# FFN up products of 512 columns with down products two tiles behind, latent-attention weight units split by halves, products on zeros at the beginning

## The reference, cut to what matters

```python
def conv_ffn(x, w_up, conv_w, conv_b, w_down):        # 2 of them, FFN_HIDDEN = 2816
    u = x @ w_up                                       # [256, 1024] @ [1024, 2 * 2816]
    up = jnp.pad(u, ((0, 0), (half, half), (0, 0)))    # over the tokens, 3 taps
    c = conv_b
    for j in range(CONV_W):
        c = c + conv_w[j] * up[:, j:j + s]
    g, val = c[..., :FFN_HIDDEN], c[..., FFN_HIDDEN:]
    return (jax.nn.gelu(g) * val) @ w_down

def swiglu(x, w_gu, w_down):                           # 2 of them, hidden width 2752
    gate, up = jnp.split(x @ w_gu, 2, axis=-1)
    return (jax.nn.silu(gate) * up) @ w_down

def mla_mixer(x, w_dq, q_norm_g, w_uq, w_dkv, kv_norm_g, w_ukv, w_o):
    cq = rms_norm(x @ w_dq, q_norm_g)                  # latent queries, 384
    q = (cq @ w_uq).reshape(b, s, H, MLA_NOPE + MLA_ROPE)
    ckv_kr = x @ w_dkv                                 # latent keys and values, 256 + 64
    ...
    # softmax attention of 8 heads, then @ w_o
```

## Time and profile before

| | us |
|---|---|
| median of 3 runs | 1225.3 (1223.99 to 1225.78) |
| profiled execution | 1222.77 |
| its span | 1221.0 |
| TensorE busy in the span | 1170.8 (96%) |
| VectorE busy | 763.6 (63%) |
| ScalarE busy | 601.2 (49%) |

### The profile page before, as it was taken

One profiled execution on the slowest core, in us unless ns is written; L12 is line 12 of the kernel. 1 busy time (PEld: TensorE's weight loads), 2 busy tenths in 40 slices (PEclk: granted clock), 3 DMA queues, 4 the chain that ended last, 5 costly groups with the idle time before them and its releaser, 6 DMA issues.

```text
span 1221.0 us, 21499 instructions
## 1 busy us (share of the span) xinstructions
PE 1170.8 (96%) x7997; PEld 1063.0 (87%) x8011; DVE 763.6 (63%) x1070; ACT 601.2 (49%) x900; POOL 69.3 (6%) x98
## 2 busy tenths in 40 slices
PE   7999999999899989999999999999989999999997
PEld 6976999999789869999987999997977878999996
DVE  5864876776656568677767455455646756555554
ACT  5554555454555555545445434334565655334342
POOL 0201000000200020000002000001000310000000
PEclk9999999999999999999999999999999999999998
DMA  6514766566243446666554666563674015766661
GB/s 204 178 35 155 206 190 187 174 202 203 93 149 119 155 124 207 186 177 204 176 169 134 195 178 200 178 166 96 176 223 156 1 36 172 209 172 200 172 175 43
DMA packets 241058, 194.59 MB, mean 159 GB/s; under 512 B 11214, under 2 KB 223792, under 8 KB 241008
## 3 DMA queue, kind: packets, MB, share of 16 engines
q1 hardware_dynamic: 240928, 193.88, 53.3%
q10 hardware_dynamic: 80, 0.03, 0.0%
HBM read 192.84 MB, written 1.05 MB: 159 GB/s over the span
## 4 chain that ended last, share of the span: by engine, by line
PE 86%; DVE 6%; ACT 4%; DMA 2%; issue 1%; POOL 1%; SPq 0%; POOLq 0%; ACTq 0%; DVEq 0%
PE psum L584 26%; PE psum L585 25%; PE psum L586 25%; DVE lo_u L1648 1%; PE psum L1143 1%; ACT hi_u L1237 1%; DVE lo_u L1665 1%; ACT hi_u L1234 1%; POOL st L506 1%; PE psum L902 1%; PE psum L1115 1%; PE psum L815 1%; PE psum L816 1%; POOL st L503 1%; DMA raw_u<-in_cmp_v_w 1%
## 5 line engine op out<-in xcount | busy, mean ns | idle before, releaser
L584 PE MATMUL psum<-act_hi,hi_u 128*128 128x256 f32 x1712 | 486.8, 284 | 9.4 <-DVE lo_u L1648 6.0
L585 PE MATMUL psum<-act_lo,hi_u 128*128 128x256 f32 x1712 | 484.2, 283 | 0.0
L586 PE MATMUL psum<-act_hi,lo_u 128*128 128x256 f32 x1712 | 484.2, 283 | 0.0
L1665 DVE TENSOR_TENSOR lo_u<-raw_u,hi_u 128x2048 fp32r<-128x2048 f32 (+3 forms) x122 | 273.7, 2243 | 236.2 <-ACT hi_u L1243 153.3
L584 PEld LDWEIGHTS psum<-act_hi,hi_u 128*128 128x128 f32 x1712 | 326.6, 191 | 17.9 <-issue 14.3
L585 PEld LDWEIGHTS psum<-act_lo,hi_u 128*128 128x128 f32 x1712 | 326.7, 191 | 3.2
L586 PEld LDWEIGHTS psum<-act_hi,lo_u 128*128 128x128 f32 x1712 | 326.7, 191 | 0.0
L1243 ACT ACTIVATE hi_u<-raw_u 128x2048 fp32r<-128x2048 f32 x72 | 137.7, 1912 | 91.6 <-PE psum L586 81.2
L584 PE MATMUL psum<-hi_d,hid_hi 128*128 128x512 f32 (+1 forms) x352 | 138.5, 393 | 1.4 <-DVE hid_lo L1755 1.4
L585 PE MATMUL psum<-lo_d,hid_hi 128*128 128x512 f32 (+1 forms) x352 | 138.0, 392 | 0.0
L586 PE MATMUL psum<-hi_d,hid_lo 128*128 128x512 f32 (+1 forms) x352 | 137.0, 389 | 0.0
(11 more groups left out here) (245 smaller groups left out, 1201.4 us busy)
## 6 DMA issues: line engine op xcount, KB each, us to landing
raw_u<-in_ffn_w_up SPq DMA_DIRECT2D x88, 512.0 KB, 5.4
raw_d<-in_ffn_w_down SPq DMA_DIRECT2D x86, 512.0 KB, 3.5
raw_u<-in_ffn_w_gu SPq DMA_DIRECT2D x84, 512.0 KB, 5.8
raw_u<-in_diff_w_qkv SPq DMA_DIRECT2D x24, 512.0 KB, 4.6
raw_u<-in_w_in SPq DMA_DIRECT2D x24, 512.0 KB, 4.4
raw_u<-in_mla_w_o SPq DMA_DIRECT2D x8, 512.0 KB, 4.0
raw_u<-in_diff_w_o SPq DMA_DIRECT2D x8, 512.0 KB, 4.1
raw_u<-in_w_out SPq DMA_DIRECT2D x8, 512.0 KB, 4.3
```

Source lines behind the costliest of these rows:

```text
L584: pe.matmul(o, s_hi, m_hi, start=start, stop=False)
L585: pe.matmul(o, s_hi, m_lo, start=False, stop=False)
L586: return pe.matmul(o, s_lo, m_hi, start=False, stop=stop)
L1665: dve.tensor_tensor(v[0], v[1], v[2].bitcast(F32), ALU.subtract).then_inc(S("lo_u_done"), 1)
```

## The change

- **Up products.** `act_hi` and `act_lo` become halves of one tensor `act_hl`, chunk by chunk side by side. The hi weights meet both in one product of 512 columns, which fills a whole bank: hi by hi in the first 256 columns, hi by lo in the other 256 (the crossed half). The lo weights meet `act_hi` in a product of 256 columns that adds to the crossed half. ScalarE then copies the crossed half out (`cross_out`) and VectorE adds the two halves into `up_sum` in SBUF; the taps, silu and the product read `up_sum`. The bank is free for the tile two later after the sum.
- **Order.** down(t) follows up(t+2) and not up(t+1). At the end: up(20), down(18), up(21), down(19), then down(20) and down(21) for the first token half, then both for the second. Tile 21's down weights get a third slot.
- **Hidden tile.** `hid_hi` is written by ScalarE from the float32 product, no longer by VectorE as a second product; `hid_lo` of a tile is made within the next one; the down weights of a tile are split one tile later than before.
- **Latent attention.** All its units (0 to 13) are split by halves, each half as soon as it has landed (`raw_half0_`, `raw_half1_`), and TensorE begins a unit when its first half is split.
- **Beginning.** Twelve products on zeros before anything else, four between the transposes of the two token halves and six behind them.

In the diff the last two pieces are ScalarE's and VectorE's order within a tile.

```diff
-WARM = [(0, 0, 0)] + 4 * [(19, 3, 1)] + 2 * [(12, 3, 1)]
+WARM = [(0, 4, 6)] + 4 * [(19, 3, 1)] + 2 * [(12, 3, 1)]
-HALVED = sorted(FIRST + list(range(U_NV, U_HI + 1)))
+HALVED = sorted(list(range(U_F0)) + FIRST[1:] + list(range(U_NV, U_HI + 1)))
+BY_HALVES = range(U_F0)
...
+            def mm_beside(bank, n, s_hi, s_lo, m_hl, start, stop):
+                pe.matmul(psum[0:n, bank, :], s_hi, m_hl.rearrange("p a t -> p (a t)"), start=start, stop=False)
+                return pe.matmul(psum[0:n, bank, SEQ:], s_lo, m_hl[:, 0, :], start=False, stop=stop)
...
                 up(1, 1, P)
-                down(0, 0, P)
                 with pe.Fori(0, LOOPED) as b:
                     up(b * 2 + 2, 0, P)
+                    down(b * 2, 0, P)
+                    up(b * 2 + 3, 1, P)
                     down(b * 2 + 1, 1, P)
-                    up(b * 2 + 3, 1, P)
-                    down(b * 2 + 2, 0, P)
                 up(20, 0, P)
+                down(18, 0, P)
+                up(21, 1, width(f, 21))
                 down(19, 1, P)
-                up(21, 1, width(f, 21))
-                down(20, 0, P)
+                down(20, 0, P, False, [0])
                 down(21, 1, width(f, 21), True, [0])
+                down(20, 0, P, False, [1])
                 down(21, 1, width(f, 21), True, [1])
...
+            pe.wait_ge(S("zeros_set"), 1)
+            keep_warm(12)
             pe.wait_ge(S("ident_in"), 16)
...
+                    cross_out(0)
+                    if f < 2:
+                        conv_mid(0, cg)
+                        cross_out(1)
+                        act.wait_ge(S("tap_b"), at2(2 * g + 1))
+                        act.activation(gg[0:n, slot, :], cg[0:n, slot, :], ACT.Gelu_apprx_tanh).then_inc(S("gated"), 1)
+                        conv_mid(1, cv)
...
+                    act.wait_ge(S("hidden"), at(g + 1))
+                    if b is not None or g >= 2:
+                        act.wait_ge(S("used_d"), at(g - 1))
+                    act.activation(hid_hi[0:n, slot, :], hf[0:n, slot, :], ACT.Copy).then_inc(S("hid_hi_done"), 1)
...
+                    sum_up(0)
+                    if b is not None or 0 < t < 21:
+                        split_d(g - 1, b)
                     if f < 2:
+                        taps(0, cg)
+                    if n == P:
+                        sum_up(1)
+                    if b is not None or t:
+                        hidden_low(g - 1, 1 - slot, P)
```

More of the change, by code:

```diff
@@ L338, in program @@
         d_sq = junk[:].rearrange("p (b d) -> p b d", d=P)
[L339 removed]
+        d_hi, d_lo = (x[:, 0:2].rearrange("p a (c t) -> p (a c) t", t=SEQ) for x in (hi_d, lo_d))
         n_ks = ar(0, 2, NB + SEQ)
@@ L395, in load_unit @@
                 k = units[u].shape[1]
-                for k0, k1 in ((0, k // 2), (k // 2, k)):
-                    sp.dma_start(unit_view(raw_u, u)[:, k0:k1], units[u][:, k0:k1]).then_inc(S(f"raw_u{u % 2}"), 16)
+                for part, (k0, k1) in enumerate(((0, k // 2), (k // 2, k))):
+                    landed = f"raw_u{u % 2}" if u not in BY_HALVES else f"raw_half{part}_{u % 2}"
+                    sp.dma_start(unit_view(raw_u, u)[:, k0:k1], units[u][:, k0:k1]).then_inc(S(landed), 16)
             def load_up(f, t, slot, n):
@@ L703, in down @@
                     g = t + FT * f
+                    d = 2 if isinstance(t, int) and t == FT - 1 else slot
                     pe.wait_ge(S("hi_d_done"), g + 1)
@@ L711, in down @@
                             mm = mm3(psum[:, 2 * tk + c, :], hid_hi[0:n, slot, tok(tk)], hid_lo[0:n, slot, tok(tk)],
-                                     hi_d[0:n, slot, w], lo_d[0:n, slot, w], False, last)
-                    mm.then_inc(S("used_d" if TT - 1 in tiles else "first_part"), 1)
+                                     hi_d[0:n, d, w], lo_d[0:n, d, w], False, last)
+                    if TT - 1 in tiles:
+                        mm.then_inc(S("used_d"), 1)
+                    elif last:
+                        mm.then_inc(S("first_part"), 1)
                 up(0, 0, P, True)
@@ new lines, in taps @@
+                    def taps(part, buf):
+                        for tap, name in ((0, "tap_a"), (2, "tap_b")):
+                            dve.wait_ge(S("conv_mid" if tap == 0 else "tap_a"), at2(2 * g + part + 1))
+                            w = at(V_CW + (f * 3 + tap) * 44 + part * FT + t)
+                            o = slice(1, SEQ) if tap == 0 else slice(0, SEQ - 1)
+                            x = slice(0, SEQ - 1) if tap == 0 else slice(1, SEQ)
+                            dve.scalar_tensor_tensor(buf[0:n, slot, o], up_sum[0:n, slot, part, x],
+                                                     vecs[0:n, bass.ds(w, 1)], buf[0:n, slot, o],
+                                                     ALU.mult, ALU.add).then_inc(S(name), 1)
@@ new lines, in tile @@
+                    if n == P:
+                        sum_up(1)
+                    if b is not None or t:
+                        hidden_low(g - 1, 1 - slot, P)
+                    dve.wait_ge(S("gated"), at(g + 1))
+                    if f < 2:
+                        taps(1, cv)
+                        dve.wait_ge(S("tap_b"), at2(2 * g + 2))
+                        gate, val = gg[0:n, slot, :], cv[0:n, slot, :]
+                    else:
+                        dve.wait_ge(S("up_sum"), at2(2 * g + 2))
+                        r = slice(n, 2 * n) if n < P else slice(0, P)
+                        gate, val = gg[r, slot, :], up_sum[r, slot, 0 if n < P else 1, :]
```

171 lines of the change are left out of this document (88 added, 83 removed).

## The result

Four executions of the changed kernel took 1213.33 us in the median (1210.59 to 1215.52), four of the kernel before 1224.64: a ratio of 0.991 (95% interval 0.989 to 0.993), 11.3 us off where 20.2 were forecast. It is 0.3 us outside the forecast range of 1199 to 1213. The profiled execution is the longest of the four, 1215.52 with a span of 1213.6.

What follows compares the result with a forecast made beforehand. TensorE was taken as the bound, busy 1170.8 of 1221.0 us, with other engines setting the edges. Terms -15.3 + 4.4 - 1.2 - 5.7 - 2.4 = -20.2 took the median from 1225.3 to 1205 us, range 1199 to 1213.

Steps and rivals of the forecast that it cites:

- Up products: FFN up chunks: one 512- and one 256-column product replace three of 256, 0.349 for 0.360 us, 1392 chunks: -15.3 us.
- First tiles: Start of each FFN: TensorE waits for tile 2's weights, about 1.9 us convolved, 0.3 gated: together +4.4 us.
- Last tile: End of both convolved FFNs: the wait for tile 21's hid_lo shrinks to about 0.2 us: -1.2 us for the two.
- Stage edges: Between stages and at the end: the first token half is done 2.75 us ahead, so norms start earlier: -5.7 us.
- the same chain, the same counts: Edges behind convolved FFNs: would match the one behind attention, 9.2 us from square to product: -1.8 and -2.1 us.
- a down block's time more: FFN loops: later-landing down loads meet splits with about 2.75 us more before TensorE wants them, so no cost.
- Beginning: Kernel start: zeros raise the clock for the latent queries, -2.0, and halves shorten the key/value wait, -0.4: -2.4 us.
- In the loops: FFN tiles: VectorE's 7.5 us and ScalarE's 5.6 stay under the 8.33 us tile time: cost nothing.
- rival (b): FFN loops: the VectorE-ScalarE chain is longer than a tile, 8.6 us for a convolved one: 1208 to 1220; chance 0.10.
- (a): Clock rival: zeros run slow, or the clock falls in gaps or the tile 2 wait: 1207 to 1211; chance 0.14.
- (c): Up products: the 512-column product costs 0.24 us there, up term between 0 and -3.5: 1217 to 1220; chance 0.07.

Runs made afterwards that it cites:

- the table's two profiles after: The changed kernel, profiled in its first measurement and again, unedited, among the experiments: medians 1213.33 and 1213.18 us.
- the two reordered kernels: Changed kernel with every second chunk's wide and short products swapped, 1207.07 us; changed kernel with eight wide, then eight short products per half tile, 1208.21 us.
- the last kernel: Five edits together on the changed kernel, among them turned chunks, later small table loads and a reordered last projection of differential attention: 1202.28 us, ratio 0.9826.

## Why the prediction was too low

Term by term, forecast and then what the table's two profiles after show against the two before:

- **Up products**: -15.3, measured -9.7 (6.9 ns by 1392). This step failed by size, 5.6 us of the 8.9 in all. I added the pace of wide products in a row to that of short ones in a row, and took single steps at the border between up and down products as proof that mixing costs nothing. In strict alternation it costs 4 to 5 ns a chunk, as the two reordered kernels show. The bounds, 0 and -18.1, held it. By the Trainium skill's 2.5 ns beyond the columns (TensorE: Matmul & The Clock Gate, "Wait — 56ns, not 53.3ns?") one product fewer would give -3.5, an estimate. The run that takes the product apart contradicts it with 9.7; the bf16 products on zeros, every 0.216 us, do agree with it.
- **First tiles**: +4.4, measured 1.8, 1.7, 0.2 and under 0.2, together +3.8. Right, chain and size. That the table load stood wholly on the path was wrong: only 0.5 of it.
- **Last tile**: -1.2. The waits of 0.86 are now 0.19 and 0.2: -1.3. Right.
- **Stage edges**: -5.7, measured about +1.3 behind the first FFN, -1.2, -0.65 and -0.55, together -1.1. The failed step is "the same chain, the same counts": for the first FFN the chain to the square has a second input, the next stage's weight unit, which ScalarE takes first and which now lands later. I had read that SyncE's loads come later, and put it down as covered by "a down block's time more" in the loops, without following the last one across the border. For the second and third I compared with the edges behind attention and behind the mixer, where no memset of GpSimd runs beside VectorE's norm; what is missing is that difference, 0.77 and 0.67. It was there to be read in the kernel before.
- **Beginning**: -2.4, measured -3.7. 1.7 of it are the halves (forecast 0.4), by the run without them: there the first product comes at 12.13, in the changed kernel at 11.39 and 11.03, where I had put next to nothing; 1.9 is the clock (48 products in 8.5 us, forecast 8.4), though it isn't shown that the zeros are needed for it.
- **In the loops**: nothing, right. No tile waits, though the run with one tile behind shows how near rival (b) was: with the same work in another order the ring is 9.12 us.

These sum to -12.0. The spans of the two pairs of profiles differ by 10.1: differential attention and the mixer, where the clock falls, were together 1.5 us longer after, and 0.4 of the FFNs is not placed. The medians differ by 11.3, which is no closer test of the sum, since single executions lie up to 5 us apart. Up products and edges missed together: with only one of the two errors the sum would have been 1210.6 or 1209.6, inside the range. Of the rivals, (a) came true at one execution in part: the fall behind the first edge, 1.5 us; but falls of the same kind are in before too. A part of (c) came true: 7 ns of the 11 were gained, 4 were not.

## What to carry to other kernels

Price a pattern by a stretch of the same pattern: two kinds of instruction that each run at a known pace need not keep it when they alternate, and turning every second pair about was here worth half of what the whole change brought. When a result is made available earlier, list everything that its consumer's engine has queued in front, loads in flight included: an earlier result meets work that used to have time. And a split or copy that looks like padding in an in-order engine may be filling a wait: before moving it, find the ring that it closes.

## What the runs showed of the hardware

- The same 512- and 256-column fp32r products take 0.3526 us a pair in strict alternation, 0.348 when every second pair is turned about, 0.347 to 0.348 when eight of each stand in a row. Products on zeros, bf16 and 512 columns, come every 0.216; fp32r ones in a row every 0.229.
- VectorE's norm of 128x1024 took 0.75 us, 1.52 and 1.42 beside a memset on GpSimd; GpSimd's step on 128x1 took 0.19 with VectorE idle and 1.05 beside a split on VectorE.
- TensorE's clock fell to its lower level in every one of the profiles once or more, within a wait of 1.4 to 4.7 us or up to 2.2 us behind one, at changing places for the same kernel: differential attention took 120.4 us without a fall and 121.7 to 123.3 with one or more (119.5 without one in the last kernel, which has another order there). The falls over transposes and products on zeros ahead of a wait cost 0.3 to 0.4 in the kernel before, the three over real products in the first profile after 1.4 to 2.7.
